# Order of the weight splits, the adaLN products and the first products of a stage in a two-layer trunk kernel; low halves in two operations

## Chip, cores and metric

One Trainium2 chip, one core. The metric is the device time of one execution in microseconds (us), the median of the runs. All work of two layers runs in one launch: TensorE (PE) multiplies, ScalarE (ACT), VectorE (DVE) and GpSimd (POOL) do the element-wise work, SyncE (SP) issues the weight transfers.

## What is computed

Two trunk layers over 128 context tokens and 256 latent tokens, D_MODEL 1024. Cut to what matters here:

```python
def ada_modulation(cvec, w, b):
    m = jax.nn.silu(cvec) @ w + b               # (1024) @ (1024, 6144)
    return m.reshape(m.shape[0], 6, D_MODEL)

def trunk_layer(x, m, lp, ...):
    sh1, sc1, g1, sh2, sc2, g2 = (m[:, i][:, None, :] for i in range(6))
    h = rmsnorm(x, lp['norm_mix_pre']) * (1.0 + sc1) + sh1
    z = h @ lp['w_in']
    z_rwkv = dwconv3(z[..., :o0], lp['rwkv_conv'])
    gates = sigmoid(z[..., o2:])
    out_a = rwkv7_branch(z_rwkv, ...)            # two directions, 8 heads of 64
    out_b = neighbourhood / dense attention      # 8 heads
    out_c = retention_branch(...)                # 8 heads
    merged = gates[:, :, 0] * out_a + gates[:, :, 1] * out_b + gates[:, :, 2] * out_c
    x = x + g1 * rmsnorm(merged @ lp['w_out'], lp['norm_mix_post'])
    h2 = rmsnorm(x, lp['norm_ffn_pre']) * (1.0 + sc2) + sh2
    return x + g2 * rmsnorm(conv_ffn(h2, ffn_up, ffn_conv, ffn_down), lp['norm_ffn_post'])
```

## The kernel before

Activations are held transposed: 128 channels on the partitions, 386 columns of tokens (128 context, a gap of 2, 256 latent), 8 tiles `h[k]` for 1024 channels. Weights stream as blocks of 128 x 1024 floats (512 KB) in one fixed order through a ring of five slots (`ring`): SP issues the transfer of block b as soon as block b-5 has been read. A block of a product is 8 units of 128 x 128.

Products are made from two roundings. ACT writes `whi`, the block rounded to the reduced fp32r type (`split(j)`, L902, three buffers); POOL subtracts it from the block and writes the rest, `wlo`, in place over the ring slot (`low(j)`, L1607). An activation tile is split in the same way, high half on ACT, low half on DVE (`lo_of`). `three` (L456) then issues three matmuls for each unit: high by high, high by low, low by high. `dense(zi, j)` (L464) makes one output tile of 128 channels: it waits for the low half of block j (the semaphore w_lo counts one for each block) and issues 8 x 3 matmuls of 386 columns into z buffer `zi % 2`. There are two such buffers in PSUM; `opened(zi)` waits until the one of two products earlier is free.

Every engine has its own program, written out by hand in the order in which it runs; semaphores join them. A layer goes through these stages:

- *Layer start.* ACT squares the tiles of x into two buffers, and PE sums each with a matmul by ones (`sum_squares(0)`); between them stand the adaLN products. The first 16 ring blocks are the adaLN weights for shift and scale of the first norm: PE multiplies the conditioning vectors (2 columns, stationary) by 2 x 512 columns of each block into rows 32 j of PSUM, and calls `sum_squares(0)` after 13 of the blocks. ACT then makes the root, a small exponential, the four copies of adaLN rows and the split of blocks 0 to 2; DVE makes a chain of small operations for the decay rates, the reciprocal and the eight `hnorm` products, then adds the adaLN bias; `modulate` on ACT applies scale and shift to each tile and makes its high half, DVE its low half. PE makes products 0 and 1 (`dense(0, 0)`, `dense(1, 1)`; the lora inputs) tile by tile as they come.
- *Four pairs of heads* p. Each takes ten split blocks (numbers `sb_` = 2 + 10 p and on; PE calls them bb) and eight adaLN blocks that are not split. PE: five products (zb to zb+4), sums for the norm of kk, lora products, then the products zb+6, zb+7, zb+9, zb+10, zb+11 with blocks sb+5 to sb+9, with steps of the attention between them (`attend`), then the matmuls `am` and the long alternation of PE and DVE for the chunked RWKV-7 form. The adaLN products of shift, scale and gate for the rest of the layer are made here in pieces (`ada_steps`, `ada_late`), two matmuls of 512 columns for each block, and copied by ACT (`late_rows`). On ACT `split(sb_ + 7)` stands behind the root of kk and four sigmoids; on POOL `low(sb_ + 7)` stands in direction d=0 of the loop over the two directions, behind kd and Lx, and `low(sb_ + 8)`, `low(sb_ + 9)` stand behind the loop. For each direction DVE makes a scan, a product with the rates, kd times k, and three more products; the last signals til_ready.
- *Merge*: gate products and branch products, 36 blocks. *Out*: 8 products (ZO, blocks SO). *Up*: 44 products (ZU, SU) with the convolution taps and the gelu. *Down*: 8 products of 22 units. Before out and up the first product waits for its activation tiles one by one (`wait=`).

Of the kernel before, what the change touches and what calls it, by code (L numbers as in the profile page):

```python
# [20 lines left out]
F32 = mybir.dt.float32  # L21
# [6 lines left out]
P = 128  # L28
# [112 lines left out]
def trunk(nc, xin, wstream, prm_d, pk_d, cc_d, const_d, x_out, nak, nav, srw, srt):  # L141
    ctx = ExitStack()
    with ctx:
# [201 lines left out]
        with nc.Fori(0, DEPTH) as layer:  # L345
            with nc.Block() as block:
# [85 lines left out]
                def _(pe):  # L432
# [31 lines left out]
                    def dense(zi, j, src=hsp, wait=None, between=None):  # L464
                        out = opened(zi)
                        pe.wait_ge(S["w_lo"].h, j + 1)
                        for k in range(KT):
# [4 lines left out]
                            three(out, j, k, src[k], k == 0, k == KT - 1, "z_done" if k == KT - 1 else None)  # L472

# [26 lines left out]
                    def ada_late(p, i):  # L500

                        j, k = 2 * (p % 2) + i % 2, i // 2
# [3 lines left out]
                        if i % 2 == 0:  # L506
                            loaded(b)
                        mm(psz[32 * j:32 * j + 2, (ZP + ZPP * p + 19) % 2, :], cs[:, k, :], ring2[b % RING][:, i % 2, :],
                           k == 0, k == KT - 1, "z_done" if i == 2 * KT - 1 else None)
                        used[0] += i % 2  # L510

                    pe.wait_ge(S["silu_c"].h, 1)

                    for jp in range(2):
                        for k in range(KT):
# [7 lines left out]
                            if jp and k == KT // 2:  # L523
                                sum_squares(0)
                    pe.wait_ge(S["row_ready"].h, 4)
                    mod_turned(0, modr)
                    dense(0, 0, wait=("h_lo", 0))
                    dense(1, 1)

                    for p in range(PAIRS):  # L530
# [3 lines left out]
                        def ada_steps(n):  # L534
                            for _ in range(n):
                                ada_late(p, late[0])
                                late[0] += 1
# [277 lines left out]
                    for mp in range(KT // 2):  # L815
                        for i, (kind, m, b, blk_, half) in enumerate(MT):
                            zi, j = ZM + 12 * mp + i, SM + 9 * mp + blk_
                            if mp == 0 and i == 6:
                                pe.wait_ge(S["o_ready"].h, PAIRS)
                                pe.wait_ge(*at_of("no_ready", PAIRS - 1, 5))  # L820
                                pe.wait_ge(S["row_ready"].h, 4 + PAIRS)
# [8 lines left out]
                            pe.wait_ge(S["w_lo"].h, j + 1)  # L830
# [6 lines left out]
                    for m in range(KT):  # L837
                        dense(ZO + m, SO + m, gsp, None if m else ("g_lo", 0))
# [7 lines left out]
                    for i in range(2 * FT):  # L846
                        dense(ZU + i, SU + i, hsp, None if i else ("h_lo", KT))
                    for m in range(KT):
                        out = opened(ZD + m)
                        for k in range(FT):  # L850
                            un = FT * m + k
                            j = SD + un // 8
                            if un % 8 == 0 or k == 0:
                                pe.wait_ge(S["w_lo"].h, j + 1)
# [11 lines left out]
                def _(act):  # L866
# [26 lines left out]
                    def modulate(j, scale, shift):  # L893
                        for k in range(KT):
                            act.wait_ge(S["hnorm"].h, KT * j + k + 1)
# [923 lines left out]
```

## Time and profile before

| | us |
|---|---|
| median of 3 runs | 2164.68 (2159.77 to 2167.46) |
| the profiled execution | 2164.02 |
| its span | 2162.2 |
| PE busy | 1963.6 (91%) |
| DVE, ACT, POOL busy | 1013.2, 935.9, 877.0 |

Mean granted clock of PE over the span: 0.964 of full speed. The second layer begins at 1081 us of the span and repeats the first. In the timeline each row is one instruction or a run of equal ones (xN): start, length, engine, line, operation, output and input by the program's names, and in brackets how long the engine had stood idle before it and for whom. L436 is the helper of all matmuls, L870 of all ACT operations, L1252, L1258 and L1261 of DVE's, L1602 of POOL's, so the tiles tell what a row is: `ringlo<-ring,whi` is a low, `whi<-ring` a split, `psz<-hhi,whi` a matmul of a product, `ring,small` an adaLN product, `mix,const` in `psw` a sum of squares.

### The profile page before, as it was taken

The page shows a single profiled execution, that of the slowest core. Times are in us where ns is not written, and L with a number is a line of the kernel's source. Part 1 is how long each engine was busy: PE and PEld are TensorE (multiplying, and loading weights), DVE is VectorE, ACT ScalarE, POOL GpSimd, SP SyncE. Part 2 cuts the span into 40 slices and gives each one's busy share as a digit, 9 for nine tenths or more (in the row PEclk, how much of TensorE's full clock was granted, in tenths as well). Part 3 has the DMA queues.
Part 4 walks back from the last instruction along what each step waited for, and adds up shares of the span by engine and source line. Part 5 has one row for each costly group of instructions (what it writes and reads, how often), then busy time and mean ns, then how long its engine had stood idle before and what let it go on. Part 6 is the DMA issues. An engine that isn't in the chain of part 4 may idle for free.

```text
span 2162.2 us, 42001 instructions
## 1 busy us (share of the span) xinstructions
PE 1963.6 (91%) x17656; PEld 1746.3 (81%) x17656; DVE 1013.2 (47%) x1492; ACT 935.9 (43%) x1744; POOL 877.0 (41%) x466
## 2 busy tenths in 40 slices
PE   4899999999999889999549999999999997899994
PEld 0777878787999779999518778777879996899994
DVE  1574747475613246550125657464745132466401
ACT  2653545444533454443136445354544334544431
POOL 0523325160555435555215233242506553455551
PEclk9899999999999989999879999999999999899997
DMA  7314132232333223333063131323223332233331
GB/s 281 117 46 133 62 117 82 86 108 75 132 125 127 88 78 125 120 126 117 30 218 125 52 128 52 127 72 108 91 82 137 119 126 78 88 127 127 120 120 44
DMA packets 64998, 233.23 MB, mean 108 GB/s; under 512 B 7328, under 2 KB 11680, under 8 KB 63904
## 3 DMA queue, kind: packets, MB, share of 16 engines
q1 hardware_dynamic: 58464, 215.21, 29.8%
q10 hardware_dynamic: 6336, 15.24, 1.9%
q8 instruction: 142, 2.33, 0.4%
q14 instruction: 56, 0.46, 0.1%
HBM read 223.58 MB, written 6.84 MB: 107 GB/s over the span
## 4 chain that ended last, share of the span: by engine, by line
PE 39%; DVE 6%; ACT 2%; POOL 1%; DMA 1%; issue 1%; SPq 0%; ACTq 0%; DVEq 0%; POOLq 0%
PE psz L436 28%; PE psw L436 10%; DVE work L1252 3%; DMA ring<-in_w 1%; DVE work L1261 1%; POOL ringlo L1602 1%; PE psz L444 0%; ACT work L870 0%; DVE rstd L1261 0%; PE psw L444 0%; ACT hbuf L870 0%; POOL work L1602 0%; DVE work L1258 0%; DVE hlo L1252 0%; ACT hhi L870 0%
## 5 line engine op out<-in xcount | busy, mean ns | idle before, releaser
L1602 POOL TENSOR_TENSOR ringlo<-ring,whi 128x1024 fp32r<-128x1024 f32 x304 | 745.1, 2453 | 768.9 <-ACT whi L870 768.7
L436 PE MATMUL psz<-hhi,whi 128*128 128x386 f32 x1760 | 616.4, 350 | 66.8 <-DVE hlo L1252 42.9
L436 PE MATMUL psz<-hlo,whi 128*128 128x386 f32 x1760 | 605.1, 344 | 0.0
L436 PE MATMUL psz<-hhi,ringlo 128*128 128x386 f32 x1760 | 603.7, 343 | 0.0
L436 PEld LDWEIGHTS psz<-hhi,whi 128*128 128x128 f32 x1760 | 336.9, 191 | 84.8 <-issue 68.7
L436 PEld LDWEIGHTS psw<-work 64*64 64x64 f32 (+2 forms) x9024 | 320.9, 136 | 77.9 <-issue 60.9
L436 PE MATMUL psw<-work 64*64 64x64 f32 (+4 forms) x9024 | 373.6, 231 | 8.1 <-DVE work L1252 4.9
L870 ACT ACTIVATE whi<-ring 128x1024 fp32r<-128x1024 f32 x304 | 320.1, 1054 | 136.7 <-PE psz L436 133.1
L436 PE MATMUL psz<-part,whi 128*128 128x386 f32 x1344 | 353.4, 344 | 1.8 <-DVE part L1252 1.8
L436 PEld LDWEIGHTS psz<-hlo,whi 128*128 128x128 f32 x1760 | 339.5, 193 | 2.1
L436 PEld LDWEIGHTS psz<-hhi,ringlo 128*128 128x128 f32 x1760 | 337.5, 192 | 0.0
L436 PEld LDWEIGHTS psz<-part,whi 128*128 128x128 f32 x1344 | 245.4, 189 | 9.1 <-DVE part L1252 1.4
L436 PE MATMUL psz<-part,ringlo 128*128 128x386 f32 x672 | 227.2, 338 | 0.0
L870 ACT ACTIVATE work<-psw 128x128 f32<-128x128 f32 (+6 forms) x320 | 122.0, 415 | 224.9 <-PE psw L436 192.1
L1252 DVE TENSOR_TENSOR work<-work 128x386 f32<-128x386 f32 (+2 forms) x184 | 194.8, 1083 | 5.0
L1258 DVE SCALAR_TENSOR_TENSOR mix<-psz,prm,mix 128x385 f32<-128x385 f32 x176 | 109.0, 620 | 140.3 <-ACT mix L870 137.2
L1602 POOL TENSOR_TENSOR work<-work 128x386 f32<-128x386 f32 (+1 forms) x48 | 46.2, 969 | 300.2 <-ACT work L870 289.5
L870 ACT ACTIVATE work<-psz 128x386 f32<-128x386 f32 (+2 forms) x176 | 84.6, 500 | 180.6 <-PE psz L436 175.6
L1261 DVE RECIPROCAL rstd<-rstd 128x386 f32<-128x386 f32 x8 | 20.5, 2564 | 267.4 <-ACT rstd L870 267.4
L870 ACT ACTIVATE mix<-psz,prm 128x386 f32<-128x386 f32 x88 | 51.4, 584 | 204.4 <-DVE mix L1252 105.1
L436 PEld LDWEIGHTS psz<-part,ringlo 128*128 128x128 f32 x672 | 126.3, 188 | 0.0
L1252 DVE TENSOR_TENSOR work<-psw,work 128x256 f32<-128x256 f32 (+3 forms) x128 | 46.0, 396 | 162.9 <-PE psw L436 162.9
(97 smaller groups left out, 1610.8 us busy)
## 6 DMA issues: line engine op xcount, KB each, us to landing
ring<-in_w SPq DMA_DIRECT2D x400, 512.0 KB, 3.4
pk<-in_pk ACTq DMA_DIRECT2D x8, 832.0 KB, 4.5
out_x<-work ACTq DMA_DIRECT2D x2, 1544.0 KB, 7.9
work<-out_x ACTq DMA_DIRECT2D x2, 1544.0 KB, 7.0
const<-in_const SPq DMA_DIRECT2D x1, 1923.0 KB, 7.4
work<-in_x SPq DMA_DIRECT2D x1, 1544.0 KB, 10.3
out_x<-work SPq DMA_DIRECT2D x1, 1544.0 KB, 5.1
out_nak<-work ACTq DMA_DIRECT2D x8, 64.0 KB, 3.1
```

The source lines that it names most:

```text
L436: ins = nc.tensor.matmul(out, a, b, start=start, stop=stop, skip_group_check=True)
L870: L.do(nc.scalar.activation(out, src, f, **kw), S[sig] if sig else None, free)
L1252: L.do(V.tensor_tensor(out, a, b, op), *sig_of(sig, free))
L1258: L.do(V.scalar_tensor_tensor(out, a, s_, b, op0, op1), *sig_of(sig, free))
L1261: L.do(V.reciprocal(out, a), *sig_of(sig, None))
L1602: L.do(G.tensor_tensor(out, a, b, op), S[sig] if sig else None)
```

## The change

- The low half of a block is made by two POOL operations of 512 columns. Each signals w_lo, and all readers wait for twice the count; none reads a half.
- `dense2` makes the first two products of a stage together, two units for each activation tile: at the layer start (0 and 1), at out (ZO, ZO+1) and at up (ZU, ZU+1).
- `ada_late` makes four matmuls of 256 columns for each block instead of two of 512, into four row groups; the weights are laid out for it on the host, `late_rows` makes four copies, and the wait for row_ready counts accordingly.
- `sum_squares(0)` stands before all adaLN products on PE.
- On ACT splits 0 and 1 stand before `modulate` and split 2 inside it, after three tiles. `split(sb_ + 7)` stands behind the copy of nk, ahead of the root of kk.
- On POOL `low(sb_ + 7)` stands ahead of the loop over directions, `low(sb_ + 8)` in it behind Lx of d=1, `low(sb_ + 9)` behind it.

```diff
+                    def dense2(zi, j, src, wait):
+
+                        out = [opened(zi), opened(zi + 1)]
+                        pe.wait_ge(S["w_lo"].h, 2 * j + 4)
+                        for k in range(KT):
+                            pe.wait_ge(S[wait[0]].h, wait[1] + k + 1)
+                            for i in range(2):
+                                three(out[i], j + i, k, src[k], k == 0, k == KT - 1, "z_done" if k == KT - 1 else None)
...
-                        j, k = 2 * (p % 2) + i % 2, i // 2
+                        j, k = i % 4, i // 4
...
-                        mm(psz[32 * j:32 * j + 2, (ZP + ZPP * p + 19) % 2, :], cs[:, k, :], ring2[b % RING][:, i % 2, :],
-                           k == 0, k == KT - 1, "z_done" if i == 2 * KT - 1 else None)
-                        used[0] += i % 2
-
+                        mm(psz[32 * j:32 * j + 2, (ZP + ZPP * p + 19) % 2, 0:256], cs[:, k, :],
+                           ring2[b % RING][:, j // 2, 256 * (j % 2):256 * (j % 2) + 256],
+                           k == 0, k == KT - 1, "z_done" if i == 4 * KT - 1 else None)
+                        used[0] += j == 3
+
+                    sum_squares(0)
                     pe.wait_ge(S["silu_c"].h, 1)
...
-                            if jp and k == KT // 2:
-                                sum_squares(0)
                     pe.wait_ge(S["row_ready"].h, 4)
                     mod_turned(0, modr)
-                    dense(0, 0, wait=("h_lo", 0))
-                    dense(1, 1)
+                    dense2(0, 0, hsp, ("h_lo", 0))
...
-                        dense(ZO + m, SO + m, gsp, None if m else ("g_lo", 0))
+                        if m > 1:
+                            dense(ZO + m, SO + m, gsp)
+                        elif m == 0:
+                            dense2(ZO, SO, gsp, ("g_lo", 0))
...
-                        dense(ZU + i, SU + i, hsp, None if i else ("h_lo", KT))
+                        if i > 1:
+                            dense(ZU + i, SU + i)
+                        elif i == 0:
+                            dense2(ZU, SU, hsp, ("h_lo", KT))
...
-                    def modulate(j, scale, shift):
+                    def modulate(j, scale, shift, block=None):
                         for k in range(KT):
+                            if block and k == 3:
+                                split(block)
...
-                        for i in range(2):
-                            j, q = 2 * (p % 2) + i, p // 2
+                        for j in range(4):
                             r = slice(32 * j, 32 * j + 2)
-                            run(modr2[r, 512 * q:512 * q + 512], psz[r, zi % 2, :], sig=None if i else "row_ready",
-                                free=zi if i else None)
+                            run(modr2[r, 256 * p:256 * p + 256], psz[r, zi % 2, 0:256], sig=None if j == 3 else "row_ready",
+                                free=zi if j == 3 else None)
...
-                    for j in range(3):
+                    for j in range(2):
                         split(j)
                     act.wait_ge(S["mod_ready"].h, 1)
-                    modulate(0, scale1, 0)
+                    modulate(0, scale1, 0, 2)
...
                         act.dma_start(nak[layer, p], nk[:, 0:P]).then_inc(S["out_k"].h, 16)
+                        split(sb_ + 7)
...
                         run(gr, z(zb + 5), free=zb + 5)
-                        split(sb_ + 7)
...
-                        tt(wlo[a], ring[:, a * 1024:(a + 1) * 1024], whi[j % 3].bitcast(F32), ALU.subtract, sig="w_lo")
+                        for i in range(2):
+                            part_ = slice(512 * i, 512 * i + 512)
+                            tt(wlo[a][:, part_], ring[:, a * 1024 + 512 * i:a * 1024 + 512 * i + 512],
+                               whi[j % 3][:, part_].bitcast(F32), ALU.subtract, sig="w_lo")
...
                         tt(bias, bias, cv("colmask", 64).unsqueeze(1).to_broadcast([P, 12, 64]), ALU.add, sig="bias_ready")
+                        low(sb_ + 7)
                         for d in range(2):
...
-                            if d == 0:
-                                low(sb_ + 7)
+                            if d:
+                                low(sb_ + 8)
...
-                        for j in (sb_ + 8, sb_ + 9):
-                            low(j)
+                        low(sb_ + 9)
```

## Rows read from the trace of the kernel before

**Rows 1.** Waits: who waited for whom, us in total, times, longest.

```profile
PE psw L436 <- DMA ring<-in_w: 61.9, 20, 31.5
PE psz L436 <- POOL ringlo L1602: 23.8, 9, 3.5
```

**Rows 2.** Stretches: busy us (instructions) of each engine, clock, DMA share, GB/s.

```profile
1651.00:1783.00 132.00, 131.76 (x750) 131.44 (x748) 38.34 (x59) 43.55 (x58) 74.48 (x32) 1.00 0.38 124
...
1311.00:1314.00 3.00, 3.00 (x12) 2.55 (x11) 2.45 (x3) 0.48 (x3) 2.52 (x3) 0.54 0.02 5
```

**Rows 3.** Timeline of the second layer's start: start, us, engine, line, what.

```profile
1086.16 0.92 ACT L870 ACTIVATE mix<-work 128x386 f32<-128x386 f32 x2
...
1109.27 3.16 PE L436 MATMUL psw<-ring,small 128*2 128x512 f32 x8 [3.00 <-DMA ring<-in_w]
...
1112.36 6.60 PE L436 MATMUL psw<-mix,const 128*128 128x386 f32 x16
...
1118.89 2.74 PE L436 MATMUL psw<-ring,small 128*2 128x512 f32 x12
1119.30 0.58 ACT L870 ACTIVATE rstd<-psw,small 128x386 f32<-128x386 f32 x1
...
1127.19 3.86 DVE L1252 TENSOR_TENSOR hbuf<-work,rstd 128x386 f32<-128x386 f32 x8
...
1131.59 0.99 ACT L870 ACTIVATE hbuf<-hbuf,small 128x128 f32<-128x128 f32 x2 [4.77 <-DVE small L1258]
...
1149.29 0.58 ACT L870 ACTIVATE work<-psz,prm 128x386 f32<-128x386 f32 x1 [2.71 <-PE psz L436]
```

**Rows 4.** Timeline of the first layer's start, PE and ACT.

```profile
37.33 1.03 PE L436 MATMUL psw<-ring,small 128*2 128x512 f32 x4 [0.24 <-DMA ring<-in_w]
...
57.07 0.98 ACT L870 ACTIVATE hbuf<-hbuf,small 128x128 f32<-128x128 f32 x2 [1.26 <-DVE small L1258]
```

**Rows 5.** Timeline of pair 1, second layer, DVE, POOL, PE; last the splits' group.

```profile
1296.77 4.10 DVE L1252 TENSOR_TENSOR work<-work 128x386 f32<-128x386 f32 x2
...
1307.74 5.37 DVE L1252 TENSOR_TENSOR work<-work 128x386 f32<-128x386 f32 x2
...
1304.67 1.17 POOL L1602 TENSOR_TENSOR work<-work 128x386 f32<-128x386 f32 x1
...
1310.16 0.41 PE L436 MATMUL psz<-hhi,whi 128*128 128x386 f32 x1 [2.50 <-POOL ringlo L1602]
...
1322.87 2.34 PE L436 MATMUL psw<-work 128*64 128x128 f32 x66
...
L870 ACT ACTIVATE whi<-ring 128x1024 fp32r<-128x1024 f32 x304 | 320.1, 1054 | 136.7 <-PE psz L436 133.1 <-DMA ring<-in_w 3.4
```

**Rows 6.** Timeline of pair 3's end, second layer: PE and ACT.

```profile
1614.90 2.94 PE L436 MATMUL psw<-work 64*64 64x64 f32 x96
...
1615.53 1.21 ACT L870 ACTIVATE work<-psz 2x512 f32<-2x512 f32 x2 [0.91 <-PE psz L436]
```

**Rows 7.** POOL's lows (ns min/median/max) and its bias operation (busy us, mean ns).

```profile
L1602 POOL TENSOR_TENSOR ringlo<-ring,whi x304: 2344/2406/5844, 56.9 to 2120.4; 128x1024 fp32r<-128x1024 f32 x152
...
L1602 POOL TENSOR_TENSOR pk<-pk,const 128x768 f32<-128x768 f32 x8 | 14.5, 1816 | 0.0
```

**Rows 8.** The chain that ended last, start of out, second layer: start, us, what.

```profile
1779.15 0.57 DVE work L1252
...
1783.15 5.00 PE psz L436 x27
...
1788.81 4.20 PE psz L436 x24
```

**Rows 9.** Timeline of the start of up, second layer: PE, ACT, DVE.

```profile
1850.45 0.60 PE L436 MATMUL psz<-hhi,whi 128*128 128x386 f32 x1 [0.64 <-DVE hlo L1252]
...
1857.06 0.58 ACT L870 ACTIVATE mix<-psz,prm 128x386 f32<-128x386 f32 x1 [3.79 <-PE psz L436]
...
1857.67 1.27 DVE L1258 SCALAR_TENSOR_TENSOR mix<-psz,prm,mix 128x385 f32<-128x385 f32 x2 [4.05 <-ACT mix L870]
```

More of the change, by code:

```diff
@@ L465, in dense @@
                         out = opened(zi)
-                        pe.wait_ge(S["w_lo"].h, j + 1)
+                        pe.wait_ge(S["w_lo"].h, 2 * j + 2)
                         for k in range(KT):
@@ L505, in ada_late @@
                             opened(ZP + ZPP * p + 19)
-                        if i % 2 == 0:
+                        if j == 0:
                             loaded(b)
-                        mm(psz[32 * j:32 * j + 2, (ZP + ZPP * p + 19) % 2, :], cs[:, k, :], ring2[b % RING][:, i % 2, :],
-                           k == 0, k == KT - 1, "z_done" if i == 2 * KT - 1 else None)
-                        used[0] += i % 2
+                        mm(psz[32 * j:32 * j + 2, (ZP + ZPP * p + 19) % 2, 0:256], cs[:, k, :],
[3 more added lines that the diff above has]
+                    sum_squares(0)
                     pe.wait_ge(S["silu_c"].h, 1)
@@ L534, in ada_steps @@
                         def ada_steps(n):
-                            for _ in range(n):
+                            for _ in range(2 * n):
                                 ada_late(p, late[0])
@@ L820, in _ @@
                                 pe.wait_ge(*at_of("no_ready", PAIRS - 1, 5))
-                                pe.wait_ge(S["row_ready"].h, 4 + PAIRS)
+                                pe.wait_ge(S["row_ready"].h, 4 + 3 * PAIRS)
                                 last = ZP + ZPP * (PAIRS - 1) + 19
@@ L829, in _ @@
                             out = opened(zi)
-                            pe.wait_ge(S["w_lo"].h, j + 1)
+                            pe.wait_ge(S["w_lo"].h, 2 * j + 2)
                             if mp == 0:
@@ L853, in _ @@
                             if un % 8 == 0 or k == 0:
-                                pe.wait_ge(S["w_lo"].h, j + 1)
+                                pe.wait_ge(S["w_lo"].h, 2 * j + 2)
                             if m == 0:
@@ L1752 @@
         wo = units(cat([tiles(g[n][l]) for n in ("w_o_rwkv", "w_o_na", "w_o_ret")], 1).reshape(-1, P, P))
-        ada = g["ada_w"][l].reshape(8, P, 3, 2, 2, 512).transpose(2, 3, 0, 1, 4, 5).reshape(48, P, 1024)
-        seq = [ada[:16], wi[12:14]]
+        ada = g["ada_w"][l].reshape(8, P, 3, 2, 2, 512)
+        late = ada[:, :, 1:].reshape(8, P, 2, 4, 2, 256).transpose(2, 4, 0, 1, 3, 5).reshape(32, P, 1024)
+        seq = [ada[:, :, 0].transpose(2, 0, 1, 3, 4).reshape(16, P, 1024), wi[12:14]]
         for p in range(PAIRS):
             seq.append(wi[[p, 4 + p, 8 + p, 14 + p, 18 + p, 22 + p, 26 + p, 30 + p, 34 + p, 38 + p]])
-            seq.append(ada[16 + 8 * p:24 + 8 * p])
+            seq.append(late[8 * p:8 * p + 8])
         for m in range(0, 8, 2):
```

## The prediction

> **What bounds the kernel now.** I read the PE waits first, then stretches, then the timeline and the chain at the places where PE waits. PE is busy for 91% of the span, so only few places can give anything. [rows 1] name two: PE waits 61.9 us for ring loads (adaLN weights, at the layer starts) and 23.8 us for low halves of weight blocks, 9 times with 3.5 us as the longest; the third is the wait for h at the start of a stage. In the merge, 131.8 of 132 us are PE work [rows 2]; up, down and merge are bound by the count of matmuls, which the change leaves alone. A "low" is POOL's making of one `wlo` block.
>
> *Layer start* [rows 3]. ACT makes two squares at 1086.2 and is then held, because PE takes up `sum_squares(0)` only after 13 adaLN blocks, at 1112.4. That takes 6.6 us, three blocks follow until 1121.6, and only behind the root at 1119.3 does the serial part start: root, the 24-wide DVE chain, reciprocal, eight `hnorm`, shift and scale. `modulate` starts at 1131.6, ten us after the last adaLN matmul. ACT sees the second product at 1149.3. Layer 0 has the same picture: block 13 at 37.3, `modulate` at 57.1 [rows 4].
>
> *Pair* [rows 5]. While low(sb+7) runs, two DVE multiplies take 4.10 us; while low(sb+8) and low(sb+9) run, two take 5.37 us; alone one takes about 0.56. DVE and POOL take turns, each instruction waiting for the other's whole one. PE waits 2.50 us for low(sb+8) and starts `dense(zb+10)` at 1310.16, then runs 3 us at a granted clock of 0.54 (the 1.2 GHz level) [rows 2], after an idle stretch; it stands at the `am` matmuls at 1322.87.
>
> **The change part by part** (the sum is made against the profiled execution: 2164.0 us, span 2162.2, 0.7 us under the median of the runs).
>
> *1. sum_squares(0) ahead of adaLN.* The squares can run from 1086.2 with their matmuls: 6.6 us as in [rows 3], up to 8 at the low clock. The root is done near 1094 and everything that hung on it (from the root's end, 1119.9, to the last `hnorm`, 1131.05, 11.2 us) lies beside the loads. Price: adaLN starts some 4 us later. The loads, not PE, set its pace: blocks 1 to 12 come at about 1.7 us each (20.4 us for 12) while PE needs 0.91 per block (2.74 for three). The first five slots are full when PE comes, so only the first release moves, by about 2 us, and SP's queue with it. I put the end of adaLN at 1110.6 (block 12) + 1.5 + 3 x 1.5 + 1 = 1117.6. Then the last two row copies, transposes and DVE's shift and scale: 2.8 us, `mod_ready` at 1120.4. Behind that ACT still has splits 0 and 1, 1.05 us each [rows 5], which wait for ring blocks 16 and 17 beside the 1.5 MB store of x; I take 1 us: `modulate` at 1121.4 instead of 1131.6, a gain of 10.2 us; layer 0 the same way 8.9 (48.2 for 57.1). Sum 19.1. Bounds: if all 4 us of delay stay and blocks 16 to 18 come 3 us late behind the store, 2 x 5 = 10; if nothing is delayed, 2 x 12 = 24.
>
> *2. dense2 at the layer start and split(2) inside modulate.* Now z(1) is complete 17.7 us after `modulate` starts. With two blocks fed by each h tile, PE follows `modulate`: 8 x 1.43 + 1.05 for split(2), + 0.6 for the last h_lo, + 1.06 for six matmuls = 14.2 us. But both z buffers are then full: the next product waits for a tap on ACT (0.58) and two on DVE (1.27) [rows 9], 1.95 us, and the clock may drop once. Gain 17.7 - 16.2 = 1.5, less 0.7 for the clock: 0.8 x 2 = 1.6.
>
> *3. Splits and lows in a pair.* split(sb+7) goes ahead of the root of kk on ACT; root, sigmoids, POOL's kd, DVE's reciprocal and scan stand queued behind it: +1 us on the DVE chain. It issues no DMA. low(sb+7) fills POOL's idle time before kd and leaves the two multiplies of d=0: their 4.10 become about 2.1. So til_ready of d=0 comes about 1 us earlier net (1302.2 for 1303.2). For d=1: kd 1.3, Lx 1.15 (as now, 1304.67 + 1.17), one DVE multiply 0.5, then low(sb+8) with 2.5 and one DVE step between its halves: ready at 1308.4 +/- 0.4. PE wants it at 1307.66: a wait of 0.75 instead of 2.50. DVE then ends d=1 near 1309.8 instead of 1313.1, so the scores in the middle of `dense(zb+10)` find s_ready, and the slow clock should go. low(sb+9) ends about 1313.7, when PE wants it (1308.4 + 2.1 + 0.95 + 2.1). What is late next is PE itself: two products 8.5 (48 x 0.177), two attends 1.8, flips 0.4 = 10.7, so `am` at 1319.1 instead of 1322.87. Taken with a margin of 0.3 for the tight low(sb+9): 3.5 us x 8 pairs = 28. Bounds: 1 us per pair (low(sb+8) half a us from now's time and slow clock kept) = 8; all of 15.2 - 10.7 = 4.5 = 36. I stay near the top because nothing else waits there.
>
> *4. Halves of 512.* From the median of 2.406 us for 1024 columns and 1.816 for 768 [rows 7] a straight line gives 2.30 ns per column and 0.05 us fixed: one half 1.23, two 2.46. 304 x 0.05 = 15 us more on POOL, under its idle time (it is 41% busy). On the path only low(sb+8) and the first lows of a layer: some 0.1 us each, in the above. No reader uses a half, so their whole use is that DVE gets in between. If the turn doesn't go to DVE there, low(sb+8) ends 0.5 earlier and DVE 0.5 later: nothing on balance.
>
> *5. ada_late as 4 x 256 columns.* 64 blocks, each 8 matmul instructions instead of 4, over the same columns. Three adaLN blocks in 2.74 us are 0.228 per instruction, of which 512 columns at 2.4 GHz are 0.213: 0.015 fixed. 4 x 0.015 x 64 = 4 us, all taken as path (PE is the bound engine); I take 3.5. Bounds: 0 and, if an instruction cost the same whatever its columns, 58 (the rival below). The nearest row, 96 instructions of 64 columns in 2.94 us (0.031 each) [rows 6], speaks for the small end. late_rows: four copies instead of two; two take 1.21 [rows 6], four at most 0.4 more in all if the fixed part is 0.2; ACT idles 1.5 us just behind. Nothing.
>
> The Trainium skill, TensorEngine Tiling (Array Packing), Tiling Modes, has 128x32 as four tiles that can load and multiply in parallel. By that rule four column groups in turn would overlap. The trace disagrees so far: blocks that alternate two groups run at 0.91 us for 4 x 512 columns, which is one after the other.
>
> *6. dense2 at ZO.* PE may start only when DVE has freed the last merge product, at 1779.7 [rows 8], instead of when its matmuls are through, just before 1779.1; it then does 48 matmuls (8.5 us) without a wait: 1788.3. Now it reaches that place at 1788.2 with a wait of 0.4 for the last g_lo. Then both z buffers are full: square and gate on ACT before ZO+2, which starts at 1789.8 instead of 1788.81: a loss of 1.0 x 2 = 2.
>
> *7. dense2 at ZU.* Now the last h_lo frees PE at 1850.45, three matmuls, then 24 more, part at the low clock; ACT sees ZU+1 at 1857.06 [rows 9]. With dense2 PE works through the waits between h tiles and is done at 1852.9; 1.95 us for the taps: the next product starts at 1854.9 instead of 1856.9. Gain 2.0, less 0.5 for the clock: 1.5 x 2 = 3.
>
> **Sum:** 19.1 + 1.6 + 28 - 3.5 - 2 + 3 = 46.2 us: 2164.0 - 46.2 = 2118.
>
> **The rivals.**
> A. *The wait in the pair stays.* low(sb+8) now stands behind kd and Lx of d=1, which hang on DVE; if DVE and POOL make each other wait once more there, PE waits its 2.5 us again, just for another reason. Gain per pair 1.2 instead of 3.5: 2136. For it: my time for it is later than PE's wish. Against: the d=0 multiplies surely lose one low.
> B. *Loads take the prologue's gain.* All 4 us of late start stay, and splits 0 to 2 wait in ACT's queue ahead of `modulate` for blocks behind the x store: 10 instead of 19: 2127.
> C. *Slower: an adaLN instruction of 256 columns costs as much as one of 512.* Each block then takes 8 x 0.228 = 1.83 instead of 0.91, 64 x 0.91 = 58 us: 2164 - 50 + 58 = 2172 (-50 is the sum without item 5). Slower from 0.2 us per instruction on. Against it: the 0.031 of the 64-column ones.
> D. *Four groups overlap.* Then a block would take about 0.3: 64 x 0.6 = 38 us less: 2164 - 50 - 38 = 2076. That is what the tiling rule above would make of it.
> E. *The change doesn't do what it says:* the freed stretches are filled by other waits (DVE behind halves, taps behind full z buffers), gain under 6 us: 2160.
>
> **How the numbers follow.** Forecast 0.6; A 0.16; B 0.12; C 0.04; D 0.04; E 0.04. The range takes in the forecast's own bounds (the pairs from 2.2 to 4.2 us each, the prologues from 14 to 22: 2105 to 2132), and A and B: 2100 to 2140, leaving out C, D, E and the tails. A measurement of this kernel can tell about 0.3% (6.5 us) from no change. Faster: forecast, A, B, D and none of the others, 0.92; within 0.3%: 0.04; slower 0.04.
>
> **What would show it.** Root of the first norm before the first adaLN block; `modulate` about 4 us behind the last adaLN matmul instead of 10; no PE wait for ringlo above 1 us in a pair and `am` about 15.3 - 3.8 = 11.5 us after the end of `dense(zb+9)`; two DVE multiplies of d=0 in about 2 us; an adaLN block of 8 instructions in 0.92 to 1.0 us; ZO+2 about 1 us later and ZU+2 about 2 us earlier relative to their stage's start; merge, up and down otherwise the same length. It is wrong if low(sb+8) is still waited for by 2 us, if ring loads of a layer start end more than 4 us later, or if an adaLN block takes over 1.2 us.

## The result, and the profile after

The changed kernel takes 2093.66 us, the median of 4 runs (2092.68 to 2095.33), and the kernel before takes 2163.49 us beside it (4 runs). The ratio is 0.9678, with a 95% interval from 0.9659 to 0.9697. The profiled execution has a span of 2093.5 us, where before had 2162.2: 68.7 us less. The forecast was 2118 us with a range of 2100 to 2140, so the time lies outside the range, and the gain is 70 us where 46 were expected.

The first fence is from the page of after. In a group, the numbers behind the bar are busy us and the mean ns of one instruction, and behind the second bar stands the engine's idle time before them.

```profile
PE 1927.7 (92%) x17912; PEld 1739.7 (83%) x17912; DVE 971.2 (46%) x1492; ACT 939.4 (45%) x1760; POOL 938.2 (45%) x770
...
L1616 POOL TENSOR_TENSOR ringlo<-ring,whi 128x512 fp32r<-128x512 f32 x608 | 803.1, 1344 | 725.4 <-ACT whi L883 725.4
```

The second is PE's waits in after (us in total, times, longest), to be read beside [rows 1].

```profile
PE psw L436 <- ACT mix L883: 58.5, 4, 28.4
PE psz L436 <- DVE hlo L1266: 21.9, 3, 7.7
PE psw L436 <- DMA ring<-in_w: 14.2, 14, 3.1
PE psz L436 <- POOL ringlo L1616: 12.5, 9, 5.8
```

The wait for ring loads fell from 61.9 to 14.2 us, but most of that is a change of name: PE now comes to the squares first and waits for them, 28.4 us at the longest, in the same place between two layers where it waited 31.5 us for the ring. The wait for low halves went from 23.8 to 12.5, and its longest is no longer in a pair but at the start of the second layer (5.8).

The groups of the two kernels show something larger. The late adaLN blocks, first of before and then of after:

```profile
L436 PE MATMUL psz<-ring,small 128*2 128x512 f32 x256 | 64.4, 592 | 0.0
```

```profile
L436 PE MATMUL psz<-ring,small 128*2 128x256 f32 x512 | 37.9, 379 | 0.0
```

These are the same 64 blocks and the same columns, in twice as many matmuls, and PE is busy with them for 37.9 us instead of 64.4. The prediction had priced this edit as a loss of 3.5 us.

Where the 68.7 us come from, read from the starts of the same product in both traces:

| place | foreseen | found |
|---|---|---|
| layer starts, up to the first product of pair 0 | -20.7 | -6.0 and -9.5 = -15.5 |
| pairs, without the stretch with adaLN blocks | -28 | -25.7 |
| pairs, the stretch with the late adaLN blocks | +3.5 | -24.0 |
| into the merge | 0 | -0.6 and -1.3 = -2.0 |
| start of out, up to the start of ZO+3 | +2 | +1.7 |
| end of out to ZU+2 | -3 | -2.3 and -1.0 = -3.3 |
| sum | -46.2 | -68.8 |

Every other stretch has the same length within 0.3 us. Foreseen and found are both for the profiled executions.

The rows that answer to [rows 5], pair 1 of the second layer in after:

```profile
1249.52 1.90 DVE L1266 TENSOR_TENSOR work<-work 128x386 f32<-128x386 f32 x2
...
1258.33 2.11 DVE L1266 TENSOR_TENSOR work<-work 128x386 f32<-128x386 f32 x2
...
1256.38 3.16 POOL L1616 TENSOR_TENSOR ringlo<-ring,whi 128x512 fp32r<-128x512 f32 x2
...
1259.69 0.41 PE L436 MATMUL psz<-hhi,whi 128*128 128x386 f32 x1 [0.56 <-POOL ringlo L1616]
...
1270.87 2.34 PE L436 MATMUL psw<-work 128*64 128x128 f32 x66
```

The two multiplies of d=0 take 1.90 us instead of 4.10 and those of d=1 take 2.11 instead of 5.37. PE waits 0.56 us for low(sb+8) instead of 2.50, and is at `am` 11.2 us after the start of `dense(zb+10)`, where it took 12.7 before: the stretch at the low clock is gone (the granted clock is 1.00 from 1260 to 1263 us).

The rows that answer to [rows 3], the start of the second layer in after:

```profile
1054.26 7.58 PE L436 MATMUL psw<-mix,const 128*128 128x386 f32 x16 [28.44 <-ACT mix L883]
1061.76 4.46 PE L436 MATMUL psw<-ring,small 128*2 128x512 f32 x20
...
1062.18 0.58 ACT L883 ACTIVATE rstd<-psw,small 128x386 f32<-128x386 f32 x1
...
1079.40 7.18 PE L436 MATMUL psw<-ring,small 128*2 128x512 f32 x20 [3.05 <-DMA ring<-in_w]
...
1088.98 5.25 POOL L1616 TENSOR_TENSOR ringlo<-ring,whi 128x512 fp32r<-128x512 f32 x4 [14.69 <-ACT whi L883]
1089.84 1.06 ACT L883 ACTIVATE whi<-ring 128x1024 fp32r<-128x1024 f32 x1 [0.93 <-DMA ring<-in_w]
1090.80 0.97 ACT L883 ACTIVATE hbuf<-hbuf,small 128x128 f32<-128x128 f32 x2
1094.34 0.66 PE L436 MATMUL psz<-hhi,whi 128*128 128x386 f32 x1 [5.80 <-POOL ringlo L1616]
...
1106.76 0.45 PE L436 MATMUL psz<-hhi,whi 128*128 128x386 f32 x1 [1.46 <-DVE work L1272]
```

The root at 1062.18 comes before nearly all of adaLN, which ends at 1086.6. `modulate` starts 4.2 us behind it instead of 10. The joined product then has to wait until POOL has made the low halves of both blocks (5.25 us from 1088.98 on).

### The profile page after: what moved, and what is told of

Read it like the earlier page. It is cut to its first block and busy times, and to the rows that moved or that the text cites. A ratio compares the mean times of both kernels' runs of the same rounds, so it can differ in the third digit from the quotient of the medians.

```text
span 2093.5 us, 42833 instructions
## 1 busy us (share of the span) xinstructions
PE 1927.7 (92%) x17912; PEld 1739.7 (83%) x17912; DVE 971.2 (46%) x1492; ACT 939.4 (45%) x1760; POOL 938.2 (45%) x770
## 5 line engine op out<-in xcount | busy, mean ns | idle before, releaser
L1616 POOL TENSOR_TENSOR ringlo<-ring,whi 128x512 fp32r<-128x512 f32 x608 | 803.1, 1344 | 725.4 <-ACT whi L883 725.4
L1266 DVE TENSOR_TENSOR work<-work 128x386 f32<-128x386 f32 (+2 forms) x184 | 136.4, 766 | 5.0
L436 PE MATMUL psw<-mix,const 128*128 128x386 f32 x128 | 59.9, 590 | 58.7 <-ACT mix L883 58.5
```

The lines of the kernel that those rows point to most:

```text
L436: ins = nc.tensor.matmul(out, a, b, start=start, stop=stop, skip_group_check=True)
L1266: L.do(V.tensor_tensor(out, a, b, op), *sig_of(sig, free))
L1616: L.do(G.tensor_tensor(out, a, b, op), S[sig] if sig else None)
```

## Experiments

Times are medians, and a ratio is that to the kernel before, in runs on the same chip, with its 95% interval. "Group" below is a set of 32 output rows of the accumulator, `psz[32*j:...]`.

### Do four row groups run at the same time?

My theory after the result, G: an adaLN matmul has only 2 output rows, and matmuls of different row groups run at the same time, two before and four after. The rival, S, is the reading of the prediction: they run one after the other, and the gain is elsewhere. The first run makes item 5 alone on the kernel before (with the four copies and the layout of the weights that go with it).

```diff
-  j, k = 2 * (p % 2) + i % 2, i // 2
+  j, k = i % 4, i // 4
-  mm(psz[32 * j:32 * j + 2, ..., :], cs[:, k, :], ring2[b % RING][:, i % 2, :], ...)
+  mm(psz[32 * j:32 * j + 2, ..., 0:256], cs[:, k, :],
+     ring2[b % RING][:, j // 2, 256 * (j % 2):256 * (j % 2) + 256], ...)
```

> The kernel before with item 5 alone: four matmuls of 256 columns into four row groups for each late adaLN block, and four copies. Theory G (matmuls into different 32-row groups of PSUM run at the same time, so the number of groups in turn counts): a block takes 0.55 us instead of 0.96, a pair 3.0 us less, in all 2139 us (2136 to 2142). Theory S (the one of the prediction: blocks run one after another, only a fixed price is added): 2167 us.

Measured: 2141.87 us for 2163.55, ratio 0.9903 [0.9881, 0.9924], 22 us faster by this edit alone. In the trace each of the eight stretches with adaLN blocks is 2.5 to 3.1 us shorter (2.7 to 3.1 in after), and one other product is 2.2 us longer. S falls.

The second run has the narrow matmuls without the additional groups: four of 256 columns in the two groups of before.

```diff
-  mm(psz[32 * j:32 * j + 2, ..., :], cs[:, k, :], ring2[b % RING][:, g, :], ...)
+  cols = slice(256 * hf, 256 * hf + 256)     # hf: 0, 0, 1, 1; g: 0, 1, 0, 1
+  mm(psz[32 * j:32 * j + 2, ..., cols], cs[:, k, :], ring2[b % RING][:, g, cols], ...)
```

The shift and scale of the second norm and the gates do not come out as in the reference here (two column halves are open in the same rows of one accumulator bank at once; whether that is the reason was not tested); the amount of work is the same.

> The kernel before, each late adaLN matmul of 512 columns made as two of 256 into the same two row groups as before. Theory G: two groups in turn as before, a block stays at 0.9 to 1.05 us: 2163 to 2169 us. Rival W (it is the shorter instruction that is cheap, the groups do nothing): a block takes 0.55 us as in the changed kernel, 2139 us. Theory S: 0.96 plus 4 x 0.015, 2167 us.

Measured: 2165.91 us (10 runs), ratio 1.0009 [0.9997, 1.0022]. The width alone does nothing.

The third puts both matmuls of 512 columns into one group.

```diff
-  mm(psz[32 * j:32 * j + 2, ..., :], ...)
+  mm(psz[64 * (p % 2):64 * (p % 2) + 2, ..., :], ...)
```

Both products are added into the same two rows, which ACT then copies twice, so again the modulation of the second norm and the gates differ from the reference.

> The kernel before, both late adaLN matmuls of a block into the same row group (their sums fall on each other, so the modulation of the second norm and the two gates is computed wrongly; all instructions and sizes stay). Theory G: nothing overlaps any more, a block of four instructions takes twice as long, 1.75 us instead of 0.96, 64 blocks 51 us: 2205 to 2220 us. Theory S (nothing overlapped before): no change, 2160 to 2168 us.

Measured: 2218.47 us in one run only (its granted clock was 0.963, like that of before), 55 us more than before (2163.55).

The timeline of the four kernels at such places in the second layer, in pair 1 for the first two and in pair 0 for the last two. A row is either one block (`x4` with 512 columns, `x8` with 256) or two blocks in a row (`x8` and `x16`). Before:

```profile
1356.28 1.03 PE L436 MATMUL psz<-ring,small 128*2 128x512 f32 x4
1363.16 1.89 PE L436 MATMUL psz<-ring,small 128*2 128x512 f32 x8
```

One group:

```profile
1391.99 1.88 PE L436 MATMUL psz<-ring,small 128*2 128x512 f32 x4
1399.72 3.60 PE L436 MATMUL psz<-ring,small 128*2 128x512 f32 x8
```

Two groups, 256 columns:

```profile
1246.17 1.90 PE L436 MATMUL psz<-ring,small 128*2 128x256 f32 x16
1251.92 1.03 PE L436 MATMUL psz<-ring,small 128*2 128x256 f32 x8
```

Four groups, 256 columns:

```profile
1231.74 1.05 PE L436 MATMUL psz<-ring,small 128*2 128x256 f32 x16
1236.64 0.61 PE L436 MATMUL psz<-ring,small 128*2 128x256 f32 x8
```

A second block adds 1.72 us with one group, 0.86 with two and 0.44 with four: half and a quarter. The busy time of all 64 blocks is 118.9, 64.4 (64.7 with narrow ones) and 37.9 us; the time of the kernel follows these differences (54.5 more by busy time and 55 measured; 26.5 less and 22 measured). The starts of single records in pair 1 of the second layer, in ns, show it directly (one group from the run above, two from before, four from after; the first two rows are one block, the third is two):

```
one group   (512 columns)  1387095  1387524  1387953  1388382
two groups  (512 columns)  1363159  1363166  1363587  1363594
four groups (256 columns)  1310328  1310335  1310341  1310348  1310544  1310551  1310557  1310565
```

With one group each record starts 429 ns after the one before it (its own length in the trace is 592 ns). With two they start in pairs 7 ns apart, with four in fours.

### The order in the pairs, and the halves

Item 3 alone on the kernel before, with whole low operations.

```diff
 ACT   act.dma_start(nak[layer, p], ...)
+      split(sb_ + 7)          # was behind the copy of gr
 POOL  (bias operation)
+      low(sb_ + 7)            # was behind Lx of d = 0
       (Lx of d = 1)
+      low(sb_ + 8)            # was behind the loop over d
```

> The kernel before with item 3 alone: split and low of block sb+7 early, low(sb+8) inside the loop behind Lx of d=1, low(sb+9) behind it; lows are whole. If the order carries the gain of the pairs and the halves do nothing on balance (the prediction): 3.2 us for each pair, 2138 us (2135 to 2142), and the wait before dense(zb+10) falls from 2.5 to under 1 us. If the halves carry it: DVE stands behind whole lows in d=1, s_ready comes as late as now, PE waits in the middle of dense(zb+10): 1 to 2 us for each pair, 2148 to 2156 us.

Measured: 2139.69 us, ratio 0.9899 [0.9879, 0.9918], 23.9 us faster. In pair 1 of the second layer PE waits less than half as long as in [rows 5]:

```profile
1292.05 0.41 PE L436 MATMUL psz<-hhi,whi 128*128 128x386 f32 x1 [1.20 <-POOL ringlo L1602]
```

`dense(zb+9)` to `dense(zb+10)` goes from 7.0 to 5.7 us (from 8.0 to 5.6 in the two pairs with p = 0), and the next product to 5.35. Before, that product lost time in two different ways. In six of the eight pairs (6.8 to 6.9 us) part of its matmuls ran at the 1.2 GHz level, after PE's wait. In pair 2 of each layer (6.25 us) the clock stayed full, and PE came early enough to wait for the attention scores in the middle of the product:

```profile
1431.86 0.48 PE L436 MATMUL psw<-pk,work 64*128 64x128 f32 x2 [0.81 <-DVE small L1448]
```

With the new order neither is left. Most of the gain of item 3 is there without any halves.

Item 4 alone on the kernel before.

```diff
-  tt(wlo[a], ring[:, a * 1024:(a + 1) * 1024], whi[j % 3], ALU.subtract, sig="w_lo")
+  for i in range(2):     # columns 512 * i to 512 * i + 512
+      tt(wlo[a][:, part_], ring[...], whi[j % 3][:, part_], ALU.subtract, sig="w_lo")
```

> The kernel before with item 4 alone: every low as two operations of 512 columns, order as before. If halves do nothing on balance (the prediction): 2160 to 2167 us. Rival: DVE gets in between in d=1, s_ready comes some 2 us earlier and the wait in the middle of dense(zb+10) goes, 1 us for each pair: 2153 to 2158 us.

Measured: 2162.98 us for 2164.98, ratio 0.9996 [0.9984, 1.0008]: no difference that can be told. The trace of pair 1, second layer, shows that the turns do change and PE's wait doesn't:

```profile
1295.59 2.98 DVE L1252 TENSOR_TENSOR work<-work 128x386 f32<-128x386 f32 x2
...
1305.92 5.93 POOL L1602 TENSOR_TENSOR ringlo<-ring,whi 128x512 fp32r<-128x512 f32 x4
1306.30 3.15 DVE L1252 TENSOR_TENSOR work<-work 128x386 f32<-128x386 f32 x2
...
1309.18 0.41 PE L436 MATMUL psz<-hhi,whi 128*128 128x386 f32 x1 [2.70 <-POOL ringlo L1602]
```

DVE's multiplies take 2.98 and 3.15 us instead of 4.10 and 5.37, and PE waits 2.70 instead of 2.50: what DVE gains, low(sb+8) loses. The product behind it is 1.5 us shorter here, but 1.5 longer in pair 3, where this run has its low clock.

The kernel after with whole lows (the diff above, undone) tells what the halves are worth in the new order.

> The changed kernel with whole lows of 1024 columns (all else as changed). The prediction's view (the order carries it): within 3 us of the changed kernel, 2091 to 2097 us. Rival: with low(sb+8) inside the loop of directions the halves are needed, since three DVE steps of d=1 stand behind it: 1 us more for each pair, 2100 to 2104 us. At the start of the merge DVE makes twelve low halves of the branches; they took 5.7 us before and 12.3 us with halves, and should take about 6 again.

Measured: 2098.11 us (2091.42 to 2098.83), ratio 0.9684 [0.9667, 0.9702], 1 us above what the prediction's view allowed. The interval overlaps that of after, so the times don't separate the two. The traces do, at the places where it counts: the wait in pair 1 is 1.18 us for 0.56,

```profile
1260.01 0.41 PE L436 MATMUL psz<-hhi,whi 128*128 128x386 f32 x1 [1.18 <-POOL ringlo L1616]
```

0.6 us in each of the six pairs with p > 0 (0.6 the other way in the two with p = 0), and the way into the merge is 2.0 us longer. That makes 4.5 us for the halves. The layer starts are 1.2 us shorter without them (2.1 shorter and 0.9 longer), so that about 3 us are left by the traces (spans 2096.3 and 2093.5).

The merge start wasn't in the prediction. DVE makes twelve low halves of the branches there while POOL makes lows. Before, in the first and in the second layer:

```profile
563.51 12.42 DVE L1252 TENSOR_TENSOR part<-mix,part 128x386 fp32r<-128x386 f32 x12
...
1638.44 5.74 DVE L1252 TENSOR_TENSOR part<-mix,part 128x386 fp32r<-128x386 f32 x12
...
1640.55 10.54 POOL L1602 TENSOR_TENSOR ringlo<-ring,whi 128x1024 fp32r<-128x1024 f32 x3 [4.04 <-ACT whi L870]
```

After, in the second layer:

```profile
1570.59 12.33 DVE L1266 TENSOR_TENSOR part<-mix,part 128x386 fp32r<-128x386 f32 x12
1570.69 3.18 POOL L1616 TENSOR_TENSOR ringlo<-ring,whi 128x512 fp32r<-128x512 f32 x2 [0.43 <-ACT whi L883]
...
1583.07 0.59 PE L436 MATMUL psz<-part,whi 128*128 128x386 f32 x2 [0.32 <-DVE part L1266]
```

With whole lows there are two outcomes. In 11 of the 14 layers of the seven kernels that have them DVE needs 12.4 us, where three of its twelve operations take 2.8 us each instead of 0.56, and no low takes more than 2.8. In the other three (before and this run in the second layer, the one-group kernel in the first) DVE needs 5.74 us, and the low that met it takes 5.84 (with two more of 2.35 these are the 10.54). So the 6 us expected above came in one layer (5.74), and 12.39 in the other. With halves DVE needs 12.3 to 12.4 us in every layer, six of its operations take 1.65, no half takes more than 1.70, and PE waits 0.32 us for DVE. From the first product of the merge to the first after its first twelve, PE needs 39.9 to 40.0 us with halves, and with whole lows 40.6 in the 11 layers and 41.2 to 41.3 in the three. The halves are thus worth 0.6 to 0.7 us per layer; the rest of the 1.3 in the second layer is the rarer outcome that before happened to have there. They bring it without the new order too (39.9 in both layers of the kernel with halves alone).

### The layer start

Items 1 and 2 alone on the kernel before: `sum_squares(0)` first, `dense2(0, 0, ...)`, split(2) inside `modulate`.

```diff
+  sum_squares(0)
   pe.wait_ge(S["silu_c"].h, 1)
   ...
-  if jp and k == KT // 2:
-      sum_squares(0)
   ...
-  dense(0, 0, wait=("h_lo", 0))
-  dense(1, 1)
+  dense2(0, 0, hsp, ("h_lo", 0))
```

> The kernel before with items 1 and 2 alone: sum_squares(0) ahead of adaLN, splits 0 and 1 ahead of modulate and 2 inside it, products 0 and 1 together. The trace of the changed kernel gives 6.0 us for layer 0 and 9.5 for layer 1 between the end of the layer before and the first product of pair 0: 2148 us (2145 to 2151). The prediction had 20.7: 2143. If part of it came from other items: above 2153.

Measured: 2145.23 us, ratio 0.9906 [0.989, 0.9922]; the span is 2147.0, 15.2 us less than before. The layer starts are 6.3 and 10.0 us shorter; of the other stretches one of the first pair is 1.7 us longer and the one into the second merge 0.7 shorter. The profiled execution was the slowest of the four (2148.80 us); by the medians the gain is 19.8 us (17 to 24 by the interval), so the times alone don't exclude the 20.7 of the prediction, and that it is less rests on the traces of the layer starts.

Three further runs ask why the traces don't show the 20.7 us of the prediction. First, the store of x is moved out of the way of the two ring blocks that splits 0 and 1 need.

```diff
-  act.dma_start(x_out, xres).then_inc(S["x_st"].h, 16)
   for j in range(2):
       split(j)
   act.wait_ge(S["mod_ready"].h, 1)
   modulate(0, scale1, 0, 2)
+  act.dma_start(x_out, xres).then_inc(S["x_st"].h, 16)
```

> The kernel after with one move: the 1.5 MB store of x is issued behind modulate instead of ahead of splits 0 and 1. Theory C (the store holds up ring blocks 16 and 17, so that modulate starts later than mod_ready allows): modulate starts 1.5 us earlier in layer 0 (its split(1) waited 1.59 us for its block, 0.29 for split(0)) and 0.9 us in layer 1 (0.93 us waited), first product of pair 0 as much: 2.4 us in all, 2091.3 for 2093.7. Rival P (the blocks are late because PE, busy with the sum of squares, released their slots late; the store has no part in it): no change, 2093.7, with the same waits of 1.6 and 0.9 us. Rival Q (the store, moved into the loads for pair 0, delays those): 1 to 3 us slower.

Measured: 2091.2 us (2089.95 to 2093.4), ratio 0.9658 [0.9645, 0.9671], which isn't told apart from after. In the trace `modulate` starts 1.4 us earlier in the first layer, but 0.65 us of that is already there in the row copies, which stand ahead of the store in both kernels, and the first product of pair 0 in the second layer is not earlier (counted from the end of the first), and split(1) still waits for its block, 1.06 us in the first layer. So the store can have a part in it and is not the whole: the blocks are late in themselves.

Second, the joined product is undone in the kernel after.

```diff
-  dense2(0, 0, hsp, ("h_lo", 0))
+  dense(0, 0, wait=("h_lo", 0))
+  dense(1, 1)
```

> The kernel after with the first two products of a layer made one after the other, as before, instead of tile by tile together; all else as after. Theory D2 (the joined product follows modulate, so that its second half isn't left over): the first product of pair 0 starts 2 us later per layer, 1.5 at least: 2097 to 2098. Rival L (the joined product has to wait for the low halves of both blocks, 5.8 us in layer 1, and gains nothing by then; a plain first product can start 2.5 us earlier on the first block alone): no change or up to 1 us faster, 2092 to 2094.

Measured: 2098.11 us (2097.5 to 2100.32), ratio 0.9692 [0.9679, 0.9706]; the intervals touch. By the traces the first product of pair 0 comes 2.5 us later in the second layer (counted from the end of the first) and 0.5 earlier in the first. So the joined product seems to earn something in the second layer only; the times alone don't settle it.

Third, the 16 adaLN blocks at the layer start are put into four groups too, the second eight in a bank of their own.

```diff
-  for i in range(2):
-      mm(psw[32 * j:32 * j + 2, 1, :], cs[:, k, :], ring2[b % RING][:, i, :], ...)
+  for j in range(4):
+      mm(psw[32 * j:32 * j + 2, 1 + jp, 0:256], cs[:, k, :],
+         ring2[b % RING][:, j // 2, 256 * (j % 2):256 * (j % 2) + 256], ...)
```

> The kernel after with the 16 adaLN blocks of a layer start also made as four instructions of 256 columns in four row groups (they alternate two groups of 512 columns now), the second half of them in another bank of the accumulator and eight copies of 256 columns instead of four of 512. Theory G (four groups run at the same time): a block takes 0.55 us instead of 0.96. Theory B (ring loads set the pace there): of the 16 x 0.4 = 6.6 us per layer only the last block and a part of the first five can be seen, 0.5 to 2 us per layer, 2090 to 2092.7. Rival W (the gain is whole): 2080. Rival N (loads take all of it): 2093.7.

Measured: 2089.59 us (2089.35 to 2091.9), ratio 0.9653 [0.964, 0.9666], a little better than all that was expected short of the whole gain. The first layer's start is 4.2 us shorter than in after, the second's 1.9. The timeline of the second start shows what bounds it:

```profile
1059.38 2.34 PE L436 MATMUL psw<-ring,small 128*2 128x256 f32 x40
...
1077.66 1.04 PE L436 MATMUL psw<-ring,small 128*2 128x256 f32 x8 [0.42 <-DMA ring<-in_w]
1078.95 1.03 PE L436 MATMUL psw<-ring,small 128*2 128x256 f32 x8 [0.25 <-DMA ring<-in_w]
1080.23 1.03 PE L436 MATMUL psw<-ring,small 128*2 128x256 f32 x8 [0.24 <-DMA ring<-in_w]
```

The five full slots are through in 2.34 us, where after needs 4.46, so the fifth is given back 2.1 us earlier; from then on PE waits for a load before nearly every block, 1.3 us apart. I read this as the loss in item 1: in after, the sum of squares (7.6 to 8.6 us) and the five first blocks stand ahead of the refill, and the loads behind it have no slack. A run with the sum of squares behind the first five blocks would test it; there is none.

### The start of out, and all together

The kernel after with two products one after the other at the start of out, as before.

```diff
-  if m > 1:
-      dense(ZO + m, SO + m, gsp)
-  elif m == 0:
-      dense2(ZO, SO, gsp, ("g_lo", 0))
+  dense(ZO + m, SO + m, gsp, None if m else ("g_lo", 0))
```

> The changed kernel with the first two products of out one after another, as before. The prediction says that dense2 loses 1.0 us for each layer there; the traces give 0.85: 2 us faster than the changed kernel, 2091.5 us. If the loss there belongs to something else (halves, the wait for x): no change, 2093.7 us.

Measured: 2089.90 us (2086.57 to 2091.37), ratio 0.9646 [0.9632, 0.966], faster than after; the intervals just touch. ACT's first product of out, second layer, in after and then in this kernel:

```profile
1719.52 0.49 ACT L883 ACTIVATE mix<-psz 128x386 f32<-128x386 f32 x1 [7.17 <-PE psz L436]
```

```profile
1713.52 0.49 ACT L880 ACTIVATE mix<-psz 128x386 f32<-128x386 f32 x1 [2.37 <-PE psz L436]
```

In after ACT idles for 7.17 us and then gets two products at once. ZO+2 starts 9.4 us after ZO instead of 8.8, and ZO itself 1.0 us later; ZO+3 makes up 0.1 of it: 1.5 us per layer.

Last, this edit, the later store and the early four groups in one kernel.

> The kernel after with three edits: the out stage's first two products one after the other as before, the store of x behind modulate, and the early adaLN blocks in four groups. If the parts add up: 2093.7 - 3.8 (out, measured alone) - 2.4 - 3 = 2084.5; if the layer start is bound by ring loads whatever is done there: 2089.9.

Measured: 2087.3 us (2085.51 to 2088.0), ratio 0.9639 [0.9625, 0.9652]. That is 6.4 us under after, and the intervals don't overlap. The layer starts are 3.1 and 1.3 us shorter than in after, less than with the early groups alone (4.2 and 1.9), so the parts don't add up: 2087.3 lies between the 2084.5 of full addition and the 2089.9 of a start bound by loads whatever is done. That the later store brings nothing more because loads are the bound fits this, but is not shown.

## Why the prediction was wrong

**The step that failed is item 5**, "Three adaLN blocks in 2.74 us are 0.228 per instruction, of which 512 columns at 2.4 GHz are 0.213: 0.015 fixed", and with it the sentence in which the trace was said to disagree with tiling. The `x4` of a block in the page counts records, and each matmul leaves two: the code has two matmuls per block. One of them alone with 512 columns takes 0.86 us (1.72 for the two of a block, one group), which is about 4 x 0.213. The 0.91 per block was two such matmuls at the same time. Each record alone takes 429 ns, twice 0.213, and two ran at once, so that busy time divided by records came out near 0.213 by coincidence: the two factors cancel. In place of a loss of 3.5 us the runs show a gain: 24.0 us in the trace of after, 22 us with item 5 alone, and 118.9, 64.4 and 37.9 us of busy time with one, two and four groups. The sum was therefore off by 3.5 + 24.0 = 27.5 us, more than the whole error of 22.5 (68.7 less 46.2).

The Trainium skill, FP8 and Floating Point Precision, TensorE Precision Notes, says that a true FP32 matmul makes four passes; the 1.72 us for two of them in one group agree with that. The Trainium skill, TensorEngine Tiling (Array Packing), Tiling Modes, says that tiles of 128x32 work independently; the runs with one, two and four groups agree with it, and the prediction's "the trace disagrees so far" was wrong. Rival D had the mechanism and the wrong size: it took the blocks of before as serial, so it saved 0.6 us per block, where a block goes from 0.86 us to 0.44 (0.41 less by busy time).

There were means to see this in the trace of before. The starts of its records come in pairs 7 ns apart with 0.42 us between pairs, which no serial reading explains.

**Point by point.**
- Items 1 and 2 (-20.7, found -15.5; alone 16.3 at the layer starts, 15.2 by the spans and 19.8 by the medians): right in kind, by the traces the gain a quarter too large. The second layer is near (9.5 of 11.0). The first got 6.0 of 9.7: the end of adaLN didn't move at all there, 47.1 us in both kernels, as the sum of squares took 8.6 us and held back the refill. I had let only 2 of the 4 us of delay through, and 1 us for the ring blocks behind it; split(1) alone waited 1.6 in the first layer. This is rival B in one of the two layers. Of item 2, the product behind two full buffers waits as foreseen, 1.46 us in the second layer, where the sum had 1.95 for the taps from [rows 9].
- Item 3 (-28, found -25.7; 23.9 alone with whole lows): right, within 0.3 us per pair. d=0's multiplies 1.90 (2.1 foreseen), PE's wait 0.56 (0.75), the slow clock and the wait for the scores gone. Rival A is out.
- Item 4 (0, found about -3 in the new order, nothing that can be told alone): the turns went as described, with a use of 0.6 us in the pairs with p > 0, a like loss in those with p = 0, and a use at the merge of 0.6 to 0.7 us per layer, which was missed.
- Item 6 (+2, found +1.7): right; 3.0 by the run that takes it out. That run has 8.8 us from ZO to ZO+2 where before has 9.5, and the kernel with halves alone has the 8.8 too, so part of the loss was hidden by the halves. The reason holds: PE works the 48 matmuls without a wait (45 are in this row of the chain),

```profile
1711.29 8.21 PE psz L436 x45
```

  and then both buffers are full. `ZO` starts 1.0 us later since it needs both buffers.
- Item 7 (-3, found -3.3): right. As this stretch also varies by 1 us among kernels without the joined product (43.4 to 44.5), the better figure is the mean over the seven kernels with it against the seven without: 42.6 us for 44.0 per layer from the start of ZO+7 to that of ZU+2, 2.9 in all.
- Rival C, a fixed cost per instruction, is out: 1.0009 with twice the matmuls at the same columns. Rival E is out.

The range was set from the bounds of the items, and a little off in its sum: pairs of 2.2 to 4.2 us and layer starts of 14 to 22 give 2111 to 2135 with the other terms as they stand, not 2105 to 2132. Neither reaches 2093.66. What the range left out is a gain by item 5, whose bounds had both been taken from the serial reading (0 to +58). A bound "below nothing", which tiling offered, stood only as a rival with 0.04.

## What to carry to other kernels

Give consecutive matmuls with few output rows (2 here) different 32-row groups of the accumulator: with one, two and four groups in turn a further block took 1.72, 0.86 and 0.44 us. Splitting the columns to fill four groups cost nothing here, and without more groups it gained nothing (1.0009). Before costing an instruction from a busy time, count the records against the code, and look at their starts: records that start a few ns apart are parallel. Where loads set the pace of a stage, look at when the slots are given back, and try to keep ahead of that only what can't wait (argued from the traces here, not tested by itself). Join two products at the start of a stage only where PE would else wait between input tiles, not where it is busy anyway (out: 1.5 us lost per layer; up: 1.4 gained).

## What the hardware showed beyond what I expected

- With the early blocks in four groups PE got through them faster, and its clock at the layer start was lower. The stretches (1066 to 1081 us) of after and then of the kernel with early groups; behind the busy times stand granted clock, DMA share, GB/s:

```profile
1066.00:1081.00 15.00, 7.98 (x30) 0.78 (x30) 7.65 (x17) 1.18 (x2) 0.31 (x1) 0.90 0.93 320
```

```profile
1066.00:1081.00 15.00, 9.64 (x80) 1.10 (x80) 5.51 (x9) 1.50 (x4) 0.31 (x1) 0.61 0.92 335
```

  The clock is 0.61 on average instead of 0.90, mostly the 1.2 GHz level, and a block of four groups there takes 1.03 us as one of two groups at 2.4 GHz does (0.61 is what it takes at the full clock). The loads hide it.
- How DVE and POOL hold each other up can go two ways with the same work. At the merge start DVE's twelve operations beside whole lows took 12.4 us in 11 of 14 layers (three of them 2.8 us each, alone 0.56) and 5.74 us in the other three, where POOL's low of 2.4 us took 5.84 instead. Beside halves they took 12.3 to 12.4 us every time, no one of them more than 1.68. The size of POOL's operation set how long one DVE operation was held, not how long the twelve took. One trace of before with its 5.74 alone would have suggested that halves double DVE's time.
